# State-space stage of a hybrid decoder layer: groups pipelined four buffers deep, and its output stored with channels on rows

## The chip, the cores and the metric

The kernel runs on one core of one Trainium2 chip. The metric is the device time of one execution in microseconds (us). "TensorE" is the matrix engine (PE in the profile, PEld its weight loads), "VectorE" is DVE, "ScalarE" ACT, "GpSimd" POOL, and "SP" the queue that issues most transfers.

## What is computed

One step of a decoder layer: attention, an S5 state-space group and memory attention, each gated, then one output projection and a final norm. The change concerns the state-space part and the stage that reads its output:

```
for each of 24 groups g (16 channels, 64 complex states), 4096 positions l:
    h[l] = lam_bar[g] * h[l-1] + b_bar[g] @ u[l, g]          # complex
    y[l, g] = real(c[g] @ h[l]) + d_skip[g] * u[l, g]
s = gelu(y)                                                  # 4096 x 384
s = s * sigmoid(s @ w_glu + b_glu) * silu(gate_s)
x = x + concat(a, s, m) @ w_out ;  y_prompt = rmsnorm(x)
```

Eight sample rows (one token each) go through the same steps beside the prompt.

## The kernel before, in words

The kernel is a row of blocks, each with one program per engine, ordered by semaphores; the next block begins when all engines have ended the last. Two blocks are touched: `ssm` (L1503 to L1739) and `mix_out` (L1937 to L2234). Between them lies `sample_attend` (attention of the sample rows).

**ssm.** Positions are cut into 512 chunks of 8 (`NCH`, `STEP`), so that a scan over chunks is one VectorE instruction. For a group, TensorE turns the input (L1701: four 128x128 transposes into a bank), makes the small matrices (L1705 to L1711: one transpose, eight products 16 columns wide, one transpose of the sample rows); below this is "turn". ScalarE copies both banks out (L1674 `ut`, L1676 `sm`). VectorE builds two matrices from `sm` (L1621 to L1623, "matrices"). TensorE drives the states (L1717, L1718: two products of 512 columns, "drive"). VectorE rotates (L1629, L1630, L1632), scans (L1634) and rotates back (L1638 `cg`, L1639 `sg`). TensorE reads out (L1724 to L1732: per 128 chunks three products, then small ones for the samples). ScalarE takes the bank through Gelu (L1680 to L1682). A float32 product of one operand pair is two TensorE instructions in the profile.

The loop runs over 12 pairs of groups with two buffers of everything. In a pair each engine does its work in the same order: both turns, both matrices, both drives, both scans, both read-outs; nothing of the next pair begins before. Gelu writes into one tile `ssm_y` with positions on partitions, and SP stores all of it at the end (L1585, 6 MB, 12 KB a run). SP, in order, loads inputs (L1567, L1568), tables (L1571) and matrices (L1574) of the next pair, each behind a wait for the buffer, and in the first eight pairs also the 16 page loads of one sample (L1452, L1453). GpSimd meanwhile works for eight samples through the cached keys (`past.work`, L1455 to L1500), independently of the groups; `sample_attend` needs its result.

**mix_out** works in 8 tiles of 512 positions, in this order on every engine:

```python
            ready(0, 0)
            with engine.Fori(0, NB // 2 - 1) as i:
                ready(2 * i + 1, 1)
                project(2 * i, 0)
                ready(2 * i + 2, 0)
                project(2 * i + 1, 1)
            ready(NB - 1, 1)
```

`ready` prepares the operand of a tile: SP loads five rows of attention and memory output, the gate and y (L2019 to L2022; one buffer of each, so it waits for the previous tile's last VectorE split, L2079). TensorE turns y from positions on 64 rows to channels on 128 (L2192: 48 instructions), ScalarE copies it out into `st` (L2141, 3 times), TensorE multiplies by `w_glu` (L2200, 18 instructions), ScalarE applies the sigmoid (L2145), VectorE multiplies twice (L2073, L2075) and both split the operand into a high and a low half (L2150, L2079). `project` is 192 TensorE instructions (L2211) on a tile prepared one step earlier, and VectorE, ScalarE, GpSimd add, norm and store. In SP's order the loads of tile n+1 come behind the four x loads of tile n-1 (L2027), of which the last waits until two of that projection's four quarters are added (L2095).

Of the kernel before, what the change touches and what calls it, by code (L numbers as in the profile page):

```python
# [32 lines left out]
ACT = mybir.ActivationFunctionType  # L33
# [1469 lines left out]
def ssm(nc, c, a, ssm_prompt, ssm_sample, past):  # L1503
# [3 lines left out]

    NB = 4
    with ExitStack() as s:
# [6 lines left out]
        y = sb("ssm_y", [P, NB, STEP, WS])  # L1521
        turns = sb("ssm_turns", [P, 2, O_R])
        gp = sb("ssm_gp", [P, 2, GPW - O_R])
        u = sb("ssm_u", [P, 2, NB, SC])
        us = sb("ssm_us", [8, 2, SC])
        ut = sb("ssm_ut", [P, 2, NCH])
        sm = sb("ssm_sm", [P, 2, 2 * SC + 8])
        toep = sb("ssm_toep", [P, 2, SC])
        wj = sb("ssm_wj", [P, 2, SC])
# [15 lines left out]
        g_in = [sem("ssm_in0"), sem("ssm_in1")]  # L1545
        u_in = [sem("ssm_u_in0"), sem("ssm_u_in1")]
        turns_in = [sem("ssm_turns_in0"), sem("ssm_turns_in1")]
# [3 lines left out]
        y_done, y_out = sem("ssm_y_d"), sem("ssm_y_out")  # L1551
        tail, tail_pe, ends, stored = sem("ssm_tail"), sem("ssm_tail_pe"), sem("ssm_ends"), sem("ssm_stored")
        block = s.enter_context(nc.Block())
        u_v = c.u_chunks.rearrange("b p (g w) -> g p b w", g=G)
        z_u = c.zs[:, CU:CU + WS].rearrange("b (g c) -> g b c", c=GC)

        @block.sync
        def _(sp):
            sp.dma_start(h0in, a["state_ssm"].rearrange("o b g p r -> (o b g) (p r)").rearrange("(t q) w -> q t w", q=96)
                         .rearrange("q t (p r) -> q t p r", r=2)).then_inc(h_in, 16)  # L1560
            with nc.allow_non_contiguous_dma(reason="two columns of each group"):
                sp.dma_start(ab[:], c.ssm_gp[:, :, O_A1:O_A1 + 2].rearrange("g p w -> p g w")).then_inc(h_in, 16)
            sp.wait_ge(zeroed, 1)
            def groups(i, with_past):
                for j in range(2):
                    sp.wait_ge(sm_tr, at(2, i, j - 1))
                    sp.dma_start(u[:, j], u_v[2 * i + j]).then_inc(u_in[j], 16)  # L1567
                    sp.dma_start(us[:, j, SC - GC:SC], z_u[2 * i + j]).then_inc(u_in[j], 16)  # L1568
                for j in range(2):
                    sp.wait_ge(cg_done, at(4, i, 2 * j - 2))  # L1570
                    sp.dma_start(turns[:, j], c.ssm_gp[2 * i + j, :, 0:O_R]).then_inc(turns_in[j], 16)  # L1571
                for j in range(2):
                    sp.wait_ge(y_done, at(2, i, j - 1))
                    sp.dma_start(gp[:, j], c.ssm_gp[2 * i + j, :, O_R:GPW]).then_inc(g_in[j], 16)  # L1574
                if with_past:
                    past.load_sample(nc, sp, a, i)


            sp.wait_ge(past.p_in, 16)
            with sp.Fori(0, past.nbs) as i:  # L1580
                groups(i, True)
            with sp.Fori(past.nbs, G // 2) as i:
                groups(i, False)
            sp.wait_ge(y_out, at(2, G // 2, 0))
            sp.dma_start(c.y_chunks.rearrange("b p t f -> p b (t f)"), y[:].rearrange("p b t f -> p b (t f)")).then_inc(stored, 16)  # L1585
# [5 lines left out]
            sp.wait_ge(stored, 64)  # L1591
# [7 lines left out]
        def _(dve):  # L1599
            dve.sem_inc(cg_done, 4)  # L1600
            dve.sem_inc(small, 2)
            dve.sem_inc(turned, 4)
            dve.sem_inc(toep_done, 2)
# [12 lines left out]
            with dve.Fori(0, G // 2) as i:  # L1616
                for j in range(2):
                    g = 2 * i + j
                    dve.wait_ge(sm_done, at(2, i, j + 1))
                    dve.wait_ge(y_done, at(2, i, j - 1))  # L1620
# [40 lines left out]

        @block.scalar
        def _(act):
            act.sem_inc(sm_done, 2)
            act.sem_inc(ut_done, 2)
            act.sem_inc(y_out, 2)
            with act.Fori(0, G // 2) as i:
# [641 lines left out]
```

## Time and profile before

| | us |
|---|---|
| median of 3 runs | 4104.67 (4100.36 to 4107.49) |
| span of the profiled execution | 4106.5 |
| TensorE busy in it | 3573.2 (87%) |
| VectorE, ScalarE, GpSimd busy | 1689.6, 1011.2, 651.6 |

The page gives no time of the profiled execution beside its span; the span lies 1.8 us above the median and inside the range of the runs. Times in the rows are us from the span's start. A timeline row is: start, length, engine, line, operation, out<-in, count, and in brackets the idle time before and what ended it. PEclk is the granted share of TensorE's full clock.

### The profile page before, as it was taken

The page shows a single profiled execution, that of the slowest core. Times are in us where ns is not written, and L with a number is a line of the kernel's source. Part 1 is how long each engine was busy: PE and PEld are TensorE (multiplying, and loading weights), DVE is VectorE, ACT ScalarE, POOL GpSimd, SP SyncE. Part 2 cuts the span into 40 slices and gives each one's busy share as a digit, 9 for nine tenths or more (in the row PEclk, how much of TensorE's full clock was granted, in tenths as well). Part 3 has the DMA queues.
Part 4 walks back from the last instruction along what each step waited for, and adds up shares of the span by engine and source line. Part 5 has one row for each costly group of instructions (what it writes and reads, how often), then busy time and mean ns, then how long its engine had stood idle before and what let it go on. Part 6 is the DMA issues. An engine that isn't in the chain of part 4 may idle for free. (4 is left out here: it accounts for less than half of the span.)

```text
span 4106.5 us, 45401 instructions
## 1 busy us (share of the span) xinstructions
PE 3573.2 (87%) x14504; PEld 2549.9 (62%) x14504; DVE 1689.6 (41%) x2594; ACT 1011.2 (25%) x1823; POOL 651.6 (16%) x1265
## 2 busy tenths in 40 slices
PE   5999999999968989989999999967777775498999
PEld 4987988979844555555555555534335652376766
DVE  4122122131117657465573746527625442323232
ACT  1102111121112443434334343423201110112120
POOL 0000000000027777700000000000036630000000
PEclk9998999989977999999999999988777676698989
DMA  3232232132231121210101001032245532332422
GB/s 103 93 118 82 78 134 81 55 132 91 74 71 47 67 68 48 79 40 16 38 20 34 21 19 27 8 120 54 49 143 175 170 97 92 119 115 92 122 85 72
DMA packets 234113, 323.61 MB, mean 79 GB/s; under 512 B 100548, under 2 KB 168812, under 8 KB 232372
## 3 DMA queue, kind: packets, MB, share of 16 engines
q1 hardware_dynamic: 184436, 203.79, 17.6%
q10 hardware_dynamic: 37584, 68.48, 4.5%
q0 software_dynamic: 11904, 48.87, 3.4%
q8 instruction: 112, 1.84, 0.2%
q14 instruction: 77, 0.63, 0.0%
HBM read 221.37 MB, written 99.61 MB: 78 GB/s over the span
## 5 line engine op out<-in xcount | busy, mean ns | idle before, releaser
L1011 PE MATMUL bank<-p,vone 128*128 128x512 f32 (+1 forms) x1728 | 861.9, 581 | 10.5 <-ACT p L958 9.9
L958 ACT ACTIVATE p<-bank,ncol 128x512 f32<-128x512 f32 (+1 forms) x864 | 562.1, 651 | 815.4 <-PE bank L1028 645.7
L1027 PE MATMUL bank<-qhi,kst 128*128 128x512 f32 (+1 forms) x864 | 644.2, 746 | 14.0 <-issue 12.6
L879 DVE TENSOR_REDUCE pm<-bank 128x1 f32<-128x512 f32 (+2 forms) x864 | 516.8, 640 | 261.0 <-PE bank L998 193.0
L1011 PEld LDWEIGHTS bank<-p,vone 128*128 128x128 f32 x1728 | 320.9, 198 | 73.6 <-issue 13.1
L478 DVE CAST whi<-wraw 128x3072 fp32r<-128x3072 f32 (+2 forms) x32 | 52.1, 1629 | 755.9 <-PE bank L539 755.9
L998 PE MATMUL bank<-kone,qone 66*128 66x512 f32 (+2 forms) x864 | 293.6, 412 | 59.8 <-DVE qlo L865 33.9
L539 PE MATMUL bank<-xhi,whi 128*128 128x512 f32 x832 | 332.0, 399 | 6.9 <-DVE xlo L504 6.9
L1028 PE MATMUL bank<-qlo,kone 66*128 66x512 f32 (+1 forms) x864 | 335.9, 389 | 0.0
L539 PE MATMUL bank<-xhi,wlo 128*128 128x512 f32 x832 | 331.3, 398 | 0.0
L539 PE MATMUL bank<-xlo,whi 128*128 128x512 f32 x832 | 330.9, 398 | 0.0
L1027 PEld LDWEIGHTS bank<-qhi,kst 128*128 128x128 f32 x864 | 169.3, 196 | 194.3 <-issue 163.3
L1028 PEld LDWEIGHTS bank<-qlo,kone 66*128 66x128 f32 x864 | 168.9, 196 | 177.7 <-issue 170.9
L539 PE MATMUL bank<-whi,xlo 128*128 128x384 f32 (+1 forms) x768 | 278.5, 363 | 0.0
L539 PE MATMUL bank<-whi,xhi 128*128 128x384 f32 (+1 forms) x768 | 277.5, 361 | 0.0
L539 PE MATMUL bank<-wlo,xhi 128*128 128x384 f32 (+1 forms) x768 | 277.5, 361 | 0.0
L892 DVE RECIPROCAL rec<-bank 64x512 f32<-64x512 f32 x48 | 161.2, 3359 | 230.1 <-PE bank L1011 229.0
L998 PEld LDWEIGHTS bank<-kone,qone 66*128 66x128 f32 x864 | 165.6, 199 | 110.1 <-issue 49.1
L2211 PE MATMUL bank<-wo_hi,mx_hi 128*128 128x512 f32 x512 | 205.1, 401 | 0.8 <-DVE wo_raw L2117 0.8
L2211 PE MATMUL bank<-wo_lo,mx_hi 128*128 128x512 f32 x512 | 202.5, 396 | 0.0
L2211 PE MATMUL bank<-wo_hi,mx_lo 128*128 128x512 f32 x512 | 202.5, 396 | 0.0
L570 ACT ACTIVATE fstage<-bank 128x512 f32<-128x512 f32 x104 | 62.2, 598 | 508.4 <-PE bank L539 508.3
(390 smaller groups left out, 4970.7 us busy)
## 6 DMA issues: line engine op xcount, KB each, us to landing
wraw<-in_w_in SPq DMA_DIRECT2D x20, 1536.0 KB, 6.8
ssm_consts<-gp POOLq DMA_DIRECT2D x6, 3080.0 KB, 10.0
x_tok<-in_x_prompt SPq DMA_DIRECT2D x8, 2048.0 KB, 12.6
gate_t<-fstage ACTq DMA_DIRECT2D x32, 512.0 KB, 2.6
mx_x<-in_x_prompt SPq DMA_DIRECT2D x32, 512.0 KB, 3.5
out_y_prompt<-mx_xo ACTq DMA_DIRECT2D x32, 512.0 KB, 2.9
q<-q_t SPq DMA_DIRECT2D x96, 128.0 KB, 3.1
past_k<-in_cache_k POOLq DMA_DIRECT2D x64, 192.0 KB, 3.3
```

Source lines behind the costliest of these rows:

```text
L478: dve.tensor_copy(whi[:, si % 2, :, 0:w], wraw[:, :, 0:w]).then_inc(whi_done, 1)
L539: last = pe.matmul(dst, lhsT, rhs, start=(k == 0 and ws is whi and xs is xhi), stop=(k == KD - 1 and ws is wlo))
L570: act.activation(fstage[:, slot, 512 * h:512 * (h + 1)], bank[:], func, scale=1.0 if scale is None else scale).then_inc(evac_done, 1)
L879: dve.tensor_reduce(pm[:, r, ch:ch + 1], c.bank[XB + n % NPRE][:, 0:w], AX.X, ALU.max).then_inc(pre_max, 1)
L892: dve.reciprocal(rec[:], ob[HD:P, :]).then_inc(o_rec, 1)
L958: act.activation(p[:, n % 3, q0:512], c.bank[n % SB][:, q0:512], ACT.Exp, bias=ncol[:, j:j + 1]).then_inc(ex, 1)
L998: mm = pe.matmul(bank[:, 0:w], qone[:, b % QS, q], kone[:, 512 * ch:512 * ch + w], start=True, stop=True)
L1011: pe.matmul(c.bank[OB + b % 2][:, q0:512], vone[:, j, :], p[:, n % 3, q0:512], start=(j == 0), stop=(j == 4 * b + 3), skip_group_check=Tru ...
L1027: pe.matmul(bank[:, q0:512], kst[:, j * P:(j + 1) * P], qhi[:, b % QS, q0:512], start=True, stop=False)
L1028: mm = pe.matmul(bank[:, q0:512], kone[:, j * P:(j + 1) * P], qlo[:, b % QS, q0:512], start=False, stop=True)
L2211: mm = pe.matmul(c.bank[4 + 2 * (t % 2) + h][:], ms_[:, j, k, t * P:(t + 1) * P], ws_[:, k, 512 * h:512 * (h + 1)], start=(k == 0 and ws_ ...
```

## The change

In `ssm` every tile that SP fills, and those that `turn` and `matrices` make, get four buffers instead of two. The loop runs over quads, one group a step, and the engines' work of different groups is interleaved: TensorE in step g does drive(g+1), turn(g+2), read-out(g). Matrices(g+2) stand in VectorE's program between the first rotation of g and its scan. The two one-column copies (L1641, L1642) move to ScalarE. The read-out has the weights stationary, three products of 512 columns with channels on the output's rows; its Gelu goes to `yb` (two buffers), and SP stores each group (2 KB runs) into a new tensor `y_t` of shape (384, 4096). Two samples' page loads stand in each of the first four quads, one behind each odd group. `mix_out` loads `st` from `y_t` directly, in three transfers with runs of 64 values, positions inside a tile in the order (t, c) instead of (c, t); the second multiplication (L2075) restores the order, into a new tile `sn`. The transposes, the copies and the tile `mx_y` go. Core of the diff; in `ssm`, SP:

```diff
+            def quad(i, more, with_past):
+                for j in range(BUF):
+                    g = BUF * i + j
+                    sp.wait_ge(y_done, g + 1 + Y0)
+                    if more:
+                        load(g + BUF, j)
+                    sp.wait_ge(y_out, g + 1 + O0)
+                    sp.dma_start(y_v[g], yb[:, j % 2]).then_inc(y_st[j % 2], 16)
+                    if with_past and j % 2:
+                        past.load_sample(nc, sp, a, 2 * i + j // 2)
...
-            sp.dma_start(c.y_chunks.rearrange("b p t f -> p b (t f)"), y[:].rearrange("p b t f -> p b (t f)")).then_inc(stored, 16)
```

VectorE (`matrices` waits for `sm_done` of the group it is called with, by ScalarE's `take`):

```diff
+            def step(i, j, more):
+                g, q = BUF * i + j, j % 2
+                dve.wait_ge(turns_in[j], 16 * (i + 1))
+                dve.wait_ge(v_done, g + 1)
+                dve.tensor_tensor(vc[:, q], c.bank[4][:], cosT, M).then_inc(turned, 1)
+                dve.tensor_tensor(vs[:, q], c.bank[5][:], sinT, M).then_inc(turned, 1)
+                dve.wait_ge(turned, 2 * g + 2)
+                dve.tensor_tensor(vr[:, q], vc[:, q], vs[:, q], A_).then_inc(scanned, 1)
+                dve.wait_ge(y_done, g - 1 + Y0)
+                if more:
+                    matrices(g + 2, (j + 2) % BUF)
+                dve.wait_ge(scanned, 2 * g + 1)
+                dve.tensor_tensor_scan(gs[:, q], gp[:, j, O_R8 - O_R:O_R8 - O_R + 1].to_broadcast([P, NCH]), vr[:, q], 0.0, M, A_
+                                       ).then_inc(scanned, 1)
+                dve.wait_ge(small, g + 1)
+                dve.tensor_tensor(cg[:, q, 1:NCH + 1], cosT, gs[:, q], M).then_inc(cg_done, 1)
+                dve.tensor_tensor(sg[:, q, 1:NCH + 1], sinT, gs[:, q], M).then_inc(cg_done, 1)
```

ScalarE (`take` copies `ut` and `sm` out of their banks):

```diff
+            def step(i, j, more):
+                g, q = BUF * i + j, j % 2
+                if more:
+                    act.wait_ge(y_done, g - 1 + Y0)
+                    take(g + 2, (j + 2) % BUF)
+                act.wait_ge(cg_done, 2 * g + 2)
+                act.activation(hl[:, 0, bass.ds(g, 1)], cg[:, q, NCH:NCH + 1], ACT.Copy)
+                act.activation(hl[:, 1, bass.ds(g, 1)], sg[:, q, NCH:NCH + 1], ACT.Copy).then_inc(small, 1)
+                act.wait_ge(y_done, g + 1 + Y0)
+                act.wait_ge(y_st[q], 16 * (BUF // 2 * i + j // 2 + 1))
+                act.activation(vsm[:, :, bass.ds(g, 1)], c.bank[7][:, 0:8].unsqueeze(2), ACT.Copy)
+                act.activation(yst[:, bass.ds(g, 1), :], c.bank[7][0:GC, 16:24].unsqueeze(1), ACT.Gelu)
+                act.activation(yb[:, q], c.bank[6][:], ACT.Gelu).then_inc(y_out, 1)
```

TensorE:

```diff
+            def read_out(g, b):
...
+                pe.matmul(c.bank[6][:], toep[:, b], ut[:, b], start=True, stop=False)
+                pe.wait_ge(cg_done, 2 * g + 2)
+                pe.matmul(c.bank[6][:], w1, cg[:, b % 2, 0:NCH], start=False, stop=False)
+                pe.matmul(c.bank[6][:], w2, sg[:, b % 2, 0:NCH], start=False, stop=True).then_inc(y_done, 1)
+            def step(i, j, more, next_):
+                if next_:
+                    pe.wait_ge(turned, 2 * g + 2)
+                    drive(g + 1, (j + 1) % BUF)
+                if more:
+                    pe.wait_ge(sm_done, g + 1)
+                    turn(i + (j + 2) // BUF, g + 2, (j + 2) % BUF)
+                read_out(g, j)
```

In `mix_out`, SP, VectorE and TensorE:

```diff
-                sp.dma_start(yc[:], y_v[n]).then_inc(in_, 16)
+                for k in range(NKS):
+                    sp.dma_start(st[:, k].rearrange("p (t c) -> p t c", t=STEP), y_v[n, k]).then_inc(in_, 16)
...
-                    dve.tensor_tensor(sig[:, k], sig[:, k], gate[:, k], M).then_inc(s_done, 1)
+                    dve.tensor_tensor(sn[:, k].rearrange("p (c t) -> p c t", t=STEP), sig[:, k].rearrange("p (t c) -> p c t", t=STEP),
+                                      gate[:, k].rearrange("p (c t) -> p c t", t=STEP), M).then_inc(s_done, 1)
...
-                    for t in range(STEP):
-                        tr = pe.matmul(c.bank[k % 2][:, t * HD:(t + 1) * HD], yc[:, t, k * P:(k + 1) * P], c.ident[0:HD, 0:HD],
-                                       start=True, stop=True)
-                    tr.then_inc(tr_done, 1)
-                pe.wait_ge(st_done, NKS * n + NKS)
+                pe.wait_ge(in_, LOADS * n + LOADS)
+                pe.wait_ge(lo_done, at(KD, n, 0))
```

## Rows read from the trace of the kernel before

**Rows 1.** Windows: us of PE, PEld, DVE, ACT, POOL; PEclk; DMA share; GB/s.
```profile
3053.00:3387.00 334.00, 254.16 (x1303) 196.26 (x1301) 163.94 (x267) 55.58 (x138) 194.69 (x275) 0.75 0.50 146
3208.00:3235.00 27.00, 22.41 (x99) 17.26 (x100) 11.15 (x21) 4.05 (x9) 18.07 (x28) 0.62 0.56 159
3610.00:3678.00 68.00, 63.96 (x263) 48.28 (x263) 20.52 (x32) 14.02 (x23) 2.25 (x4) 0.90 0.33 105
```
**Rows 2.** Waits, 3025 to 3390 us: the read-out's (total, times, longest).
```profile
PE bank L1724 <- DVE ssm_sg L1639: 49.4, 20, 4.5
```
**Rows 3.** Timeline of POOL, state-space stage: its last instruction.
```profile
3330.90 0.21 POOL L1486 TENSOR_TENSOR past_qk<-past_k 128x12 f32<-128x12 f32 x1 [0.18 <-POOL past_k L1486]
```
**Rows 4.** Timeline: a group's turn (first, last), then VectorE's matrices (first, last).
```profile
3107.59 0.63 PE L1701 MATMUL bank<-ident,ssm_u 128*128 128x128 f32 x4 [0.42 <-issue]
...
3109.95 0.22 PE L1711 MATMUL bank<-ident,ssm_us 8*128 8x8 f32 x1
...
3110.63 0.35 DVE L1621 SCALAR_TENSOR_TENSOR ssm_toep<-ident,ssm_gp,ssm_sm 128x128 f32<-128x128 f32 x1 [1.92 <-ACT ssm_sm L1676]
...
3111.00 0.19 DVE L1623 TENSOR_SCALAR ssm_wj<-ssm_sm 128x64 f32<-128x64 f32 x1
```
**Rows 5.** Timeline after POOL's end: VectorE's scan, and TensorE's read-out that waits.
```profile
3347.44 1.22 DVE L1634 TENSOR_TENSOR_SCAN ssm_vs<-ssm_gp,ssm_vc 128x512 f32<-128x512 f32 x1
...
3350.04 0.39 PE L1724 MATMUL bank<-ssm_sm 128*128 128x8 f32 x2 [1.24 <-DVE ssm_sg L1639]
```
**Rows 6.** Groups by line, 3025 to 3390 us: busy us, mean ns.
```profile
L1634 DVE TENSOR_TENSOR_SCAN ssm_vs<-ssm_gp,ssm_vc 128x512 f32<-128x512 f32 x24 | 34.1, 1420 | 0.8
L1638 DVE TENSOR_TENSOR ssm_cg<-ssm_turns,ssm_vs 128x512 f32<-128x512 f32 x24 | 28.2, 1176 | 0.8
L1639 DVE TENSOR_TENSOR ssm_sg<-ssm_turns,ssm_vs 128x512 f32<-128x512 f32 x24 | 22.8, 948 | 0.0
...
L1621 DVE SCALAR_TENSOR_TENSOR ssm_toep<-ident,ssm_gp,ssm_sm 128x128 f32<-128x128 f32 x24 | 14.3, 595 | 147.7 <-ACT ssm_sm L1676 147.7
```
**Rows 7.** The tile ssm_y: its first and last evacuation by ScalarE.
```profile
L1682 ACT ACTIVATE ssm_y<-bank x24: 597/597/597, 3066.3 to 3381.1; 128x512 f32 x24
```
**Rows 8.** SP: a sample's 16 page loads (first, last); landing of L1574.
```profile
3106.19 0.36 SPq L1452 DMA_DIRECT2D past_v<-in_cache_v  x1
...
3119.13 0.34 SPq L1453 DMA_DIRECT2D past_lf<-in_cache_logf  x1
...
DMA to landing us min/median/max: 2.6/3.6/9.2
```
**Rows 9.** Timeline of SP: end of the state-space stage, first load of the next.
```profile
3381.68 0.41 SPq L1585 DMA_DIRECT2D y_chunks<-ssm_y  x1
...
3385.68 1.19 SPq L1589 DMA_DIRECT2D out_ssm_sample<-ssm_u  x1
3399.42 0.30 SPq L1792 DMA_DIRECT2D at_z<-z_sample  x1
```
**Rows 10.** Timeline, output stage: transposes, then GLU, between two projections.
```profile
3632.31 3.78 PE L2192 MATMUL bank<-ident,mx_y 64*128 64x64 f32 x32
...
3643.81 10.93 PE L2200 MATMUL bank<-mx_st,w_glu 128*128 128x512 f32 x18 [1.17 <-ACT mx_st L2141]
...
3651.15 0.19 PEld L2200 LDWEIGHTS bank<-mx_st,w_glu 128*128 128x128 f32 x1 [0.24 <-issue]
...
3653.72 0.19 PEld L2200 LDWEIGHTS bank<-mx_st,w_glu 128*128 128x128 f32 x1 [0.24 <-issue]
...
3654.18 0.80 PE L2211 MATMUL bank<-wo_hi,mx_hi 128*128 128x512 f32 x1
```
**Rows 11.** SP's first load for the next tile; the y tile's issue-to-landing times.
```profile
3611.48 0.38 SPq L2019 DMA_DIRECT2D mx_am<-mix_t  x1
...
DMA to landing us min/median/max: 10.7/14.9/18.8
```
**Rows 12.** Windows as in 1: transfers in runs of 256 bytes and less.
```profile
1216.00:1220.00 4.00, 1.12 (x4) 0.72 (x4) 3.59 (x7) 0.00 (x0) 3.43 (x8) 0.50 1.42 163
```

More of the change, by code:

```diff
@@ L1579, in _, with load @@
[L1579 to L1585 removed]
+            def load(g, b):
+                sp.dma_start(u[:, b], u_v[g]).then_inc(u_in[b], 16)
+                sp.dma_start(us[:, b, SC - GC:SC], z_u[g]).then_inc(u_in[b], 16)
+                sp.dma_start(gp[:, b], c.ssm_gp[g, :, O_R:GPW]).then_inc(g_in[b], 16)
+                sp.dma_start(turns[:, b], c.ssm_gp[g, :, 0:O_R]).then_inc(turns_in[b], 16)
@@ L1586, in _ @@
+            for j in range(BUF):
+                load(j, j)
+            sp.wait_ge(past.p_in, 16)
+            with sp.Fori(0, past.nbs // 2) as i:
+                quad(i, True, True)
+            for i in range(past.nbs // 2, LASTQ + 1):
+                quad(i, i < LASTQ, False)
+            for j in range(2):
+                sp.wait_ge(y_st[j], 16 * (G // 2 + 1))
             sp.dma_start(c.ys_t.rearrange("(g c) b -> c g b", c=GC), yst[:]).then_inc(stored, 16)
@@ L1644, in _ @@
+            for j in range(2):
+                matrices(j, j)
+            with dve.Fori(0, LASTQ) as i:
+                for j in range(BUF):
+                    step(i, j, True)
+            for j in range(BUF):
+                step(LASTQ, j, j < 2)
             bc = [P, 8, G]
-            dve.wait_ge(y_out, at(2, G // 2, 0))
+            dve.wait_ge(y_out, G + O0)
             dve.tensor_tensor(hn[:], h0[:], ab[:, :, 0].unsqueeze(1).to_broadcast(bc), M).then_inc(tail, 1)
@@ L1685, in _ @@
+            for j in range(2):
+                take(j, j)
+            with act.Fori(0, LASTQ) as i:
+                act.activation(table[:], c.minus_half[:, 0:1], ACT.Gelu)
+                for j in range(BUF):
+                    step(i, j, True)
+            for j in range(BUF):
+                step(LASTQ, j, j < 2)
         @block.tensor
         def _(pe):
-            pe.sem_inc(y_done, 2)
-            pe.sem_inc(sm_tr, 2)
+            pe.sem_inc(y_done, Y0)
             pe.wait_ge(prep, 6)
@@ L1733, in _, with turn @@
-            pe.wait_ge(small, at(2, G // 2, 0))
+            def turn(i, g, b):
+                pe.wait_ge(u_in[b], 32 * (i + 1))
+                pe.wait_ge(g_in[b], 16 * (i + 1))
+                for n in range(NB):
+                    tr = pe.transpose(c.bank[b % 2][:, n * P:(n + 1) * P], u[:, b, n, :], c.ident[:])
+                tr.then_inc(ut_tr, 1)
+                small_b = c.bank[2 + b % 2]
+                pe.transpose(small_b[:, 0:SC], gp[:, b, 0:SC], c.ident[:])
+                for t in range(STEP):
+                    w0 = (STEP - 1 - t) * GC
+                    pe.matmul(small_b[:, SC + t * GC:SC + (t + 1) * GC], gp[:, b, w0:w0 + SC], gp[:, b, O_CC - O_R:O_CC - O_R + GC],
+                              start=True, stop=True)
+                pe.transpose(small_b[:, 2 * SC:2 * SC + 8], us[:, b, :], c.ident[0:8, 0:8]).then_inc(sm_tr, 1)
@@ new lines, in step @@
+            def step(i, j, more, next_):
+                g = BUF * i + j
+                if next_:
[5 more added lines that the diff above has]
+                read_out(g, j)
+            for j in range(2):
+                turn(0, j, j)
+            drive(0, 0)
+            with pe.Fori(0, LASTQ) as i:
+                for j in range(BUF):
+                    step(i, j, True, True)
@@ L1734, in _ @@
+            for j in range(BUF):
+                step(LASTQ, j, j < 2, j < BUF - 1)
+            pe.wait_ge(small, G + 2)
             pe.wait_ge(tail, 4)
```

184 lines of the change are left out of this document (54 added, 130 removed).

## The prediction, made before the changed kernel was run

> **What bounds the kernel now.** I read the page first: TensorE is busy 87% of the span, so it bounds most of it, and only stretches where it waits, or does work that can go, are worth a change. The windows by stage find them. In the state-space stage TensorE is busy for 254 of 334 us at a mean granted clock of 0.75 [rows 1]: it stops and, in its busy time, often runs at the lower of its two levels (1.2 of 2.4 GHz). VectorE is busy for 164, GpSimd for 195: no engine fills the stage, a chain does. The waits name it: the read-out stands 49.4 us behind VectorE's last rotation [rows 2], because a pair runs turn, matrices, drive, scan, read-out one after the other. From the first Gelu to the last are 314.8 us for 23 groups, 13.7 each [rows 7]. GpSimd's own work ends at 3331.1 [rows 3], 50 us before the groups do, so it is hidden now and is the next floor.
>
> The stage's end shows the second place. SP issues the 6 MB store of y when all is done, and the next block's first load comes 17.7 us later [rows 9].
>
> In the output stage TensorE is busy for 94% of a tile's time [rows 1]; there each instruction taken from it is time. Between two projections lie 21.9 us: 11.5 from the first transpose to the GLU products (work and waits for ScalarE's copies), then 10.4 of GLU, whose first products run at the low clock [rows 10].
>
> **The change, part by part. The groups' loop.** It removes the pair's barriers, but the new order is a ring, not a free pipeline. Matrices(g+2) stand ahead of scan(g) in VectorE's program and need turn(g+2), which TensorE makes only after drive(g+1). One step at full clock: drive, four passes at 0.43 (six passes lie between the two weight loads of [rows 10]), 1.72; turn 2.58 [rows 4]; ScalarE's copy with its hand-offs 0.46 and matrices 0.56 [rows 4]; scan, rotation back and TensorE's start 2.60 [rows 5]; the two last 512-column products of the read-out 1.72. Together 9.64, of which 6.02 is TensorE. The rest of VectorE's step (2.1 for the forward rotation) and the product with `toep` lie beside it.
>
> Two corrections. While GpSimd works, VectorE's operations on SBUF are longer: scan 1.42 for 1.22, the rotations back 1.18 and 0.95 for 0.69, the first matrix 0.60 for 0.35 [rows 4 to 6]: 1.20 on average over 24 groups, of which some 21 fell in GpSimd's time, so 1.4 in those. And TensorE still waits in each step, at full clock for 3.62 less the first product and small ones, so the clock will not stay up. Its bounds are 1.0 and the 0.62 of the worst stretch of this stage [rows 1]; I take 0.75, the stage's own, since the new step has the same kinds of work and again a wait. Then a step is 6.02 / 0.75 + 3.62 + 1.4 = 13.0. From the first Gelu, taken to stay where it is, 21 steps of 13.0 and two short ones (no turn; no drive) of about 5 are 283, against 314.8: **32 saved**, with ends of -4 (a step of 14.7, below) and some 49 (a step under 11; GpSimd then ends the stage, below).
>
> What is moved: the two one-column copies leave VectorE for ScalarE, which idles and runs them beside the read-out: nothing. SP gets a store a group: 24 issues of about 0.4 [rows 9], and in the first 16 groups two groups cost it 16 page loads, 13.3 us [rows 8], and ten further issues, some 6: 19 of 26 us, so SP has room. But it is in order: behind an odd group's page loads the next group's inputs go out some 3 us late, and land 3.6 later, at most 9.2 [rows 8]; they are wanted about a step and a drive, 15 us, after their buffer came free. Covered at 13.0; at a step under 11 SP is the cover that goes. Gelu waits for the store two groups back, 26 us earlier: covered by the same margin. The deeper buffers cost nothing in themselves.
>
> **The stage's end.** With y stored group by group, what is left is the chain to the last store: its issue ends 5.2 after the last Gelu [rows 9], landing 3.6 (median of a 258 KB load [rows 8]): 8.8 instead of 17.7, **9 saved**, between 3 (landing 9.2) and 10 (2.6).
>
> **The output stage.** At six boundaries (tiles 2 to 7) transposes and copies go, and GLU begins where the projection ended, on an engine that had no gap: 18 passes at 0.43 are 7.7, instead of 21.9. That is 14.2 each, **85**; if GLU ran at half the clock, 15.5, it would be 38. ScalarE stores the last quarter before its first sigmoid, some 5 us after the boundary, as the copies wait now; GLU's third product needs a sigmoid at that time, so no stall of size. Tile 1 has no projection ahead of it: 11.5 of transposes go, and SP's two additional issues come on top, about 1.1: **10**. Tile 0 lies beside the splitting of the output weights on VectorE: 0, up to 11. The second multiplication reads with a stride of 64 values; VectorE is idle for two thirds of the stage [rows 1], so even twice its time is hidden.
>
> The cover of all this is the loads of tile n+1. Their first issue comes 20.8 us before the projection's end [rows 10, 11]; y is the fourth, 1.7 later, and lands 14.9 after that in the median: 4.2 to spare. The three new loads move the same 768 KB in runs of 256 bytes. I bound them by nothing, and by the 163 GB/s that short runs got elsewhere [rows 12], 4.8 us if none of it overlapped. With 1.1 for the issues this is 1.1 to 5.9 later, so between 3.1 to spare and 1.7 late. I take no wait: present y rows go to 64 partitions only, the new ones to 128, so the upper end counts a transfer that replaces one as if it were added.
>
> The Trainium skill (DMA: Bandwidth & Descriptors, Specifications) speaks against this part: under 512 bytes a run misses line rate, since the engine reads, modifies and writes. An estimate by the page, taking that as double work on the 163, is 9.6 us for y, and the sum would lose 6.5 at each of seven tiles, some 46.
>
> **Sum.** 32 + 9 + 85 + 10 = 136. The profiled span, 4106.5, lies 1.8 above the median; taken from the median, 4104.7 - 136 = **3969**.
>
> **The rivals. GpSimd becomes the end.** If the clock rises with the denser work, a step is about 11 (9.64 + 1.4) and the groups end near 3310; the block then ends with GpSimd, at 3331, or some 10 later if VectorE's denser work slows it as it now slows VectorE. The next block begins near 3342 instead of 3399.4: 58 for 41, and **3952**. It decides at a step below about 12.5. For it: TensorE's share of a step rises. Against: the wait in each step, and SP.
>
> **The ring gives nothing.** The change would then not do what it says: groups overlap in the program, but each step is as long as half a pair. At clock 0.62 the step is 6.02 / 0.62 + 3.62 + 1.4 = 14.7, the loop loses 4, the end still gains 9: **4005**. For it: a stretch at 0.62 exists, and eight instructions of 16 columns stand in every turn. Against: the barriers between pairs are gone.
>
> **Late y loads.** They take the 5.9 of the bound on top of the slowest landing so far, 18.8 for 14.9 [rows 11]: 5.6 late at tiles 1 to 7, 39 lost, **4008**. For it: the short runs. Against: 4.2 to spare in the median, and rows on 128 partitions.
>
> **Slower than before: the same loads, far later.** One mechanism: the 3072 short runs a tile drain so slowly that TensorE waits at seven boundaries for more than it saves. It decides at 136 / 7 = 19.4 us a tile behind the slack of 3.1, which is 768 KB at some 35 GB/s on top of what moves now. At 25 us: 7 x 25 - 136 = 39 lost, **4144**. For it: no row of before shows these runs from this tensor. Against: short runs at 163 GB/s [rows 12].
>
> **How the numbers follow.** Forecast 0.50, with its own range of 3953 to 3985; GpSimd's end 0.20; the ring without gain 0.15; late loads 0.10; slower 0.03; parts that cancel to within 0.2% (8 us, about what a measurement of this kernel can tell from no change) 0.02. The range takes in the first four: from 3940, where GpSimd's end has a faster tile 0 beside it, to 4015. Faster: all but the last two, 0.95.
>
> **What would show it.** Right: a Gelu every 13 us, the first rotation back directly behind matrices of two groups on; GpSimd's end still before the groups'; the next block 9 after the last Gelu; GLU products directly behind the last projection product, 7.7 long, with no wait for a DMA. Wrong: steps of 14 and more, or below 12 with GpSimd last; a wait of TensorE for `mx_st` loads of several us at each tile; ScalarE or SP as what ends the read-out's wait.

## The result, and the profile after

The changed kernel takes 3958.24 us (median of 4 runs, 3954.73 to 3964.21) against 4106.08 for the kernel before: a ratio of 0.9628, 95% interval 0.9605 to 0.9652. The forecast was 3969, with a range of 3940 to 4015. The profiled execution has a span of 3953.1 us. One execution of the last kernel below (v2_ring_pages_first) took 6225.22 us, at a granted clock of 0.77 where the others had 0.92, and is left out of its median.

First the state-space stage. The source view of the Gelu line: 24 groups, shortest, median and longest duration in ns, then first and last start.

```profile
L1698 ACT ACTIVATE ssm_yb<-bank x24: 571/571/575, 3059.0 to 3341.5; 128x512 f32<-128x512 f32 x24
```

From first to last are 282.5 us, where [rows 7] had 314.8. The 21 full steps take 272.7, or 12.99 each; the two short ones take 5.2 and 4.6. The first Gelu is also 7.3 us earlier. The windows view from first to last Gelu, columns as in [rows 1]:

```profile
3059.00:3342.00 283.00, 216.84 (x826) 121.82 (x824) 139.13 (x198) 51.53 (x168) 189.17 (x270) 0.76 0.63 185
```

TensorE is granted 0.76 of its clock and idles for 66 us. The waits of the stage (3025 to 3375; total us, times, longest) name the reason:

```profile
DVE ssm_toep L1621 <- ACT ssm_sm L1683: 152.2, 24, 7.7
...
POOL past_k L1464 <- issue: 73.7, 64, 3.2
PE bank L1749 <- DVE ssm_sg L1644: 65.9, 23, 5.0
```

The wait for the rotation back is longer than in [rows 2], not shorter. One step in the timeline shows the ring:

```profile
3161.51 1.02 PE L1737 MATMUL bank<-ssm_ut,ssm_sm 128*128 128x512 f32 x2
...
3163.77 1.86 PE L1730 MATMUL bank<-ssm_gp 128*128 128x16 f32 x16
...
3165.82 0.39 ACT L1683 ACTIVATE ssm_sm<-bank 128x264 f32<-128x264 f32 x1 [1.36 <-PE bank L1732]
...
3166.24 0.35 DVE L1621 SCALAR_TENSOR_TENSOR ssm_toep<-ident,ssm_gp,ssm_sm 128x128 f32<-128x128 f32 x1 [6.17 <-ACT ssm_sm L1683]
...
3166.71 1.22 DVE L1639 TENSOR_TENSOR_SCAN ssm_vs<-ssm_gp,ssm_vc 128x512 f32<-128x512 f32 x1
...
3168.57 0.69 DVE L1644 TENSOR_TENSOR ssm_sg<-ssm_turns,ssm_vs 128x512 f32<-128x512 f32 x1
...
3169.31 2.07 PE L1749 MATMUL bank<-ssm_cg,ssm_gp 128*128 128x512 f32 x2 [1.96 <-DVE ssm_sg L1644]
...
3171.18 1.91 PE L1750 MATMUL bank<-ssm_sg,ssm_gp 128*128 128x512 f32 x2
3172.89 1.92 PE L1737 MATMUL bank<-ssm_ut,ssm_sm 128*128 128x512 f32 x2
```

Drive, turn, ScalarE's copy, VectorE's matrices, scan, rotation, the last two products, next drive: each waits for the one before. From drive to drive this step takes 11.4 us; the operations of VectorE shown are as short in it as without GpSimd's work (see e3_no_products), and the mean of 12.99 has longer ones. VectorE stood idle for 6.17 us with a scan ready to run, because the matrices of two groups on come first in its program. The end of the stage on GpSimd, and on SP the next block's first load (timelines; answers to [rows 3] and [rows 9]):

```profile
3336.87 1.07 POOL L1486 TENSOR_TENSOR past_qk<-past_k 128x12 f32<-128x12 f32 x1 [0.18 <-POOL past_k L1486]
```

```profile
3349.18 0.29 SPq L1830 DMA_DIRECT2D at_z<-z_sample  x1
```

GpSimd ends at 3337.9, 3.6 us before the last Gelu. The next block starts 7.7 us after that Gelu (18.4 before), so 50.2 us earlier in all. The profiles of the experiments tell who ends the stage: the next block's first load comes 7.7 to 7.8 us after the last Gelu where the groups end it (here and in e3, e4, e5, e9 and e10), and 6.5 us after GpSimd's last instruction where GpSimd does (e1, e2, v1 and v2).

Then the output stage. TensorE's timeline at a boundary of steady tiles, where [rows 10] had 21.9 us:

```profile
3560.16 0.40 PE L2238 MATMUL bank<-wo_lo,mx_hi 128*128 128x512 f32 x1
3560.39 5.31 PE L2227 MATMUL bank<-mx_st,w_glu 128*128 128x512 f32 x12
3566.75 2.84 PE L2227 MATMUL bank<-mx_st,w_glu 128*128 128x512 f32 x6 [1.04 <-ACT mx_sig L2181]
3569.03 0.79 PE L2238 MATMUL bank<-wo_hi,mx_hi 128*128 128x512 f32 x1
```

GLU starts directly behind the projection and takes 8.64 us. SP's loads for it, and TensorE's waits in the whole stage (answers to [rows 11]):

```profile
3539.66 0.38 SPq L2058 DMA_DIRECT2D mx_am<-mix_t  x1
...
3541.34 10.66 SPq L2062 DMA_DIRECT2D mx_st<-y_t  x3
```

```profile
PE bank L2227 <- DMA mx_st<-y_t: 45.3, 2, 22.7
PE bank L2227 <- ACT mx_sig L2181: 7.0, 6, 1.4
```

The loads of y cause two waits, at tiles 0 and 1, and none in the steady tiles. The stage, from its first load to the end of the span, is 102.4 us shorter.

### The profile page after: what moved, and what is told of

Its sections match the earlier page's. It is cut to its first block and busy times, and to the rows that moved or that the text cites. A ratio compares the mean times of both kernels' runs of the same rounds, so it can differ in the third digit from the quotient of the medians.

```text
span 3953.1 us, 43519 instructions
## 1 busy us (share of the span) xinstructions
PE 3467.9 (88%) x13688; PEld 2412.2 (61%) x13688; DVE 1684.8 (43%) x2546; ACT 984.9 (25%) x1833; POOL 657.1 (17%) x1265
## 5 line engine op out<-in xcount | busy, mean ns | idle before, releaser
L1011 PE MATMUL bank<-p,vone 128*128 128x512 f32 (+1 forms) x1728 | 863.6, 581 | 10.7 <-ACT p L958 10.1
L998 PE MATMUL bank<-kone,qone 66*128 66x512 f32 (+2 forms) x864 | 293.7, 412 | 59.6 <-DVE qlo L865 33.6
L998 PEld LDWEIGHTS bank<-kone,qone 66*128 66x128 f32 x864 | 166.2, 200 | 109.5 <-issue 50.2
```

The costliest lines, as they stand in the source:

```text
L998: mm = pe.matmul(bank[:, 0:w], qone[:, b % QS, q], kone[:, 512 * ch:512 * ch + w], start=True, stop=True)
L1011: pe.matmul(c.bank[OB + b % 2][:, q0:512], vone[:, j, :], p[:, n % 3, q0:512], start=(j == 0), stop=(j == 4 * b + 3), skip_group_check=Tru ...
```

## The experiments

My theory after the result: the new order of the groups, a ring of 13.0 us, carries the gain of the state-space stage, with GpSimd as the floor just below. Its rivals: the deeper buffers carry it; or the ring sets nothing. For the output stage: the loads are hidden in steady tiles, with 2 to 3 us to spare. All times of the stage in one table; "first to last" is the Gelu's first and last start, and the waits are counted between them. Three more profiles with the changed kernel's state-space stage (e5, e6 and e7 below) have 284.5, 285.1 and 282.0 us from first to last, so a difference of some 3 us in that column tells nothing. A time marked * is a single run.

| kernel | first to last, us | TensorE's waits for `ssm_gp` loads | time of the kernel, us |
|---|---|---|---|
| before | 314.8 | 4.1 | 4106.1 |
| changed | 282.5 | none of size | 3958.2 |
| pairs, four buffers (e1_pairs) | 266.9 | none of size | 3953.4 |
| pairs, four buffers, first products late (e10_toep_late) | 283.4 | none of size | 3963.8* |
| pairs, two buffers (e9_two_buffers) | 318.0 | 22.6 | 3989.3* |
| matrices last (e2_matrices_last) | 229.1 | 25.3 | 3956.4 |
| no GpSimd products (e3_no_products) | 260.5 | none of size | 3936.7* |
| both (e4_both) | 233.0 | 32.1 | 3904.3* |
| matrices last, early page numbers (v1_ring_pages) | 239.0 | 33.6 | 3913.0 |

**The order alone undone (e1_pairs).** On TensorE, and likewise on the other engines:

```diff
-                for j in range(BUF):
-                    step(i, j, True, True)
+                for j in range(0, BUF, 2):
+                    for x in range(2):
+                        turn(i, BUF * i + j + x, j + x)
+                    for x in range(2):
+                        drive(BUF * i + j + x, j + x)
+                    for x in range(2):
+                        read_out(BUF * i + j + x, j + x)
```

> Only the pipelining is undone: each engine again works through a pair of groups (transposes of both, drives of both, scans of both, read-outs of both); the four buffers, the earlier loads, the store per group and the new output stage stay. Theory (the order of the steps carries the gain of the stage): first Gelu at 3059 as in the changed kernel, then 315 us to the last as in the kernel before, so the last at 3374 and the next block 32 us later: 3958 + 32 = 3990 us, from 3985 to 3995. Rival (the deeper buffers and earlier loads carry half of it): 299 us from first to last Gelu, 3974 us.

It is not slower: 3953.41 us, ratio 0.9614 (0.9596 to 0.9633), where the theory had 3990. The interval overlaps that of the changed kernel; the difference shows in the stage. Its Gelu line, its window from first to last Gelu, and its waits in the same stretch:

```profile
L1696 ACT ACTIVATE ssm_yb<-bank x24: 571/571/572, 3059.2 to 3326.1; 128x512 f32<-128x512 f32 x24
```

```profile
3059.00:3327.00 268.00, 216.29 (x848) 123.69 (x848) 154.33 (x201) 52.80 (x172) 184.04 (x259) 0.82 0.64 195
```

```profile
DVE ssm_toep L1621 <- ACT ssm_sm L1681: 92.1, 22, 7.6
...
PE bank L1751 <- DVE ssm_sg L1642: 22.6, 15, 2.6
```

The changed kernel's wait for the rotation back, also from first to last Gelu:

```profile
PE bank L1749 <- DVE ssm_sg L1644: 64.7, 22, 5.0
```

TensorE is busy as long as in the changed kernel (216.3 for 216.8 us), but waits for the rotation back 22.6 us instead of 64.7. So the pipelined order costs 15.6 us of the stage against pairs; it does not gain. Both theory and rival fall: the old order with the rest of the change is faster than either had it. The last Gelu comes 15.4 us earlier than in the changed kernel, the next block's first load only 4.7 (3344.5), because GpSimd then ends the stage, at 3338.1.

**The ring broken (e2_matrices_last).**

```diff
-                dve.wait_ge(y_done, g - 1 + Y0)
-                if more:
-                    matrices(g + 2, (j + 2) % BUF)
                 dve.wait_ge(scanned, 2 * g + 1)
...
                 dve.wait_ge(small, g + 1)
+                dve.wait_ge(y_done, g - 1 + Y0)
                 dve.tensor_tensor(cg[:, q, 1:NCH + 1], cosT, gs[:, q], M).then_inc(cg_done, 1)
                 dve.tensor_tensor(sg[:, q, 1:NCH + 1], sinT, gs[:, q], M).then_inc(cg_done, 1)
+                if more:
+                    matrices(g + 2, (j + 2) % BUF)
```

> VectorE makes the matrices of group g+2 after the second product of group g instead of ahead of its scan, so that the scan no longer waits for ScalarE's copy of the small matrices. Theory (the ring over TensorE, ScalarE and VectorE sets 13.0 us a step, and GpSimd, done at 3336.9, is the floor just below it): a step falls to 8 to 11 us, the last Gelu comes by 3310 or sooner, the wait of the scan for ScalarE (152 us) goes, and the block then ends with GpSimd at 3337 to 3345, so the next block's first issue comes 0 to 9 us earlier: 3949 to 3958 us. Rival (the ring does not set the step; TensorE's clock, SP's queue or the DMA engines do): steps stay at 12.5 to 13 and the time at 3958.

Ratio 0.9620 (0.9607 to 0.9633), 3956.40 us: inside the theory's band, as are the step and the last Gelu. Its Gelu line, the waits from first to last Gelu, and GpSimd's last instruction:

```profile
L1698 ACT ACTIVATE ssm_yb<-bank x24: 571/571/575, 3063.1 to 3292.2; 128x512 f32<-128x512 f32 x24
```

```profile
DVE ssm_toep L1621 <- ACT ssm_sm L1683: 69.4, 19, 11.2
...
PE bank L1723 <- DMA ssm_gp<-ssm_consts: 25.3, 8, 7.1
...
PE bank L1749 <- DVE ssm_sg L1642: 1.7, 1, 1.7
```

```profile
3346.29 0.21 POOL L1486 TENSOR_TENSOR past_qk<-past_k 128x12 f32<-128x12 f32 x1 [0.18 <-POOL past_k L1486]
```

TensorE's wait for the rotation falls from 64.7 to 1.7 us, a step from 13.0 to 10.4 (21 steps in 218.1 us). VectorE's wait for the copy does not go, though the theory had it gone (69.4 us), but TensorE no longer waits behind it. The last Gelu comes 49 us earlier, and the kernel gains nothing that can be told, because GpSimd now ends the stage, at 3346.5. Most of its later end is a later start: its first transfer of the stage is issued at 3032.1 in this profile and at 3025.7 in the changed kernel's. From there to its end it takes 314.4 us, for 312.3 there and 309.0 to 311.2 in e5, e6 and e7. The next block's first load comes 3.8 us later than in the changed kernel's profile (3353.0), not earlier. The next wait is the one for `ssm_gp` loads, 8 times: SP issues them behind 16 page loads.

**GpSimd's products and sums left out, alone and with the ring broken (e3_no_products, e4_both).**

```diff
-                pool.tensor_tensor(k, k, self.q[:].unsqueeze(1).to_broadcast([P, CP, WF]), ALU.mult).then_inc(self.summed, 1)
+                pool.sem_inc(self.summed, 1)
+                pool.wait_ge(pace, 3 * b + ch * 3 // NCK + 1)
...
-                    pool.tensor_tensor(out, kv[:, :, :, 0:w], kv[:, :, :, w:2 * w], ALU.add).then_inc(self.summed, 1)
+                    pool.sem_inc(self.summed, 1)
```

> Left out: GpSimd's products and sums over the cached keys (the scores are set to zero); its page loads stay, paced by the groups. Theory (contention with GpSimd's tensor operations costs VectorE's part of the ring 1.4 us a step): a step takes 11.6 us, the last Gelu is at 3059 + 21 x 11.6 + 10 = 3313, the scan takes 0.95 us again instead of 1.2, and the time is 28 us less, 3930. Rival (no contention on the path): steps stay at 13, 3958 us.

> Both edits together: matrices after the second product, and GpSimd's products and sums left out. Theory: with neither the ring nor GpSimd, a step is TensorE's own 6.02 / 0.75 = 8.0 us or the DMA engines' time for a group's loads (busy 0.73 of 13 us, so some 9.5), hence 8 to 10 us a step, the last Gelu at 3240 to 3280 and the time at 3860 to 3900. Rival (something else holds the step, as SP's queue): steps of 11 us or more, over 3915.

Without GpSimd's products and sums a step takes 11.93 us (21 steps in 250.5; 11.6 expected) and the one run 3936.74 us (3930 expected), so contention costs 1.06 a step where the prediction had 1.4. VectorE's groups of the changed kernel from first to last Gelu (count, busy us, mean ns, idle before), and those of e3_no_products:

```profile
L1639 DVE TENSOR_TENSOR_SCAN ssm_vs<-ssm_gp,ssm_vc 128x512 f32<-128x512 f32 x23 | 28.0, 1215 | 0.2
L1643 DVE TENSOR_TENSOR ssm_cg<-ssm_turns,ssm_vs 128x512 f32<-128x512 f32 x23 | 25.6, 1113 | 0.8
L1644 DVE TENSOR_TENSOR ssm_sg<-ssm_turns,ssm_vs 128x512 f32<-128x512 f32 x23 | 25.5, 1108 | 0.0
```

```profile
L1641 DVE TENSOR_TENSOR_SCAN ssm_vs<-ssm_gp,ssm_vc 128x512 f32<-128x512 f32 x23 | 28.1, 1220 | 0.2
L1645 DVE TENSOR_TENSOR ssm_cg<-ssm_turns,ssm_vs 128x512 f32<-128x512 f32 x23 | 15.9, 693 | 0.8
L1646 DVE TENSOR_TENSOR ssm_sg<-ssm_turns,ssm_vs 128x512 f32<-128x512 f32 x23 | 15.8, 686 | 0.0
```

In the ring it is the two rotations back that GpSimd lengthens (1113 for 693, 1108 for 686 ns); the scan does not change, though the expectation said it would. The Trainium skill (SBUF — State Buffer, SBUF: two separate sides) has the two engines take turns at a shared port pair that one of them holds for a whole instruction. The trace agrees for the rotations back, which read two tiles of SBUF; the forward products, which read a bank, take 680 and 677 ns beside GpSimd's work and 684 and 682 without. Which operation is lengthened goes with the order of the work, though: with the ring broken the scan is slower beside GpSimd too (e2_matrices_last, then e4_both):

```profile
L1636 DVE TENSOR_TENSOR_SCAN ssm_vs<-ssm_gp,ssm_vc 128x512 f32<-128x512 f32 x22 | 33.3, 1514 | 0.8
```

```profile
L1638 DVE TENSOR_TENSOR_SCAN ssm_vs<-ssm_gp,ssm_vc 128x512 f32<-128x512 f32 x22 | 26.9, 1224 | 0.7
```

With both edits a step is 10.7 us and the last Gelu starts at 3290.7, where the theory had 8 to 10 and 3240 to 3280; it was too low, and the rival's 11 or more is not reached either. The groups are no faster than with the ring broken alone (233.0 us for 229.1 in all), so GpSimd does not set that pace; but its floor is gone, and the kernel drops to 3904.3, just above the band expected. What is left of the step there shows in the waits: 32.1 us for `ssm_gp` loads.

**The buffers undone, and the earlier loads with them (e9_two_buffers).** e1_pairs with `BUF = 2`, each load behind the event that it had before (inputs after the turn, tables after the rotation, matrices after the read-out), and ahead of ScalarE's copies and VectorE's matrices the waits for an earlier read-out that two buffers need.

> The pairs of e1_pairs with two buffers of every tile again, and the loads where the kernel before has them (inputs behind the turn, tables behind the rotation back, matrices behind the read-out). Read-out, output and stores stay new. Theory after e1_pairs (the read-out's new form carries the gain of the stage: behind VectorE's last rotation stand two products of 512 columns instead of twelve of 128 columns and the small ones): the buffers are worth little, first to last Gelu 267 to 275 us as in e1_pairs (266.9). Rival (the deeper buffers and earlier loads carry it): 300 to 315 us, as in the kernel before.

The rival is the nearer one: 318.0 us, 3 above its band, and 3 above the kernel before, which has the old read-out. With two buffers, then, the rest of the new stage gains nothing. Its Gelu line, its window, its wait, and TensorE and SP around the end of one pair:

```profile
L1709 ACT ACTIVATE ssm_yb<-bank x24: 570/570/571, 3056.4 to 3374.4; 128x512 f32<-128x512 f32 x24
```

```profile
3056.00:3375.00 319.00, 253.66 (x849) 153.01 (x848) 146.30 (x201) 63.07 (x184) 188.96 (x274) 0.72 0.57 168
```

```profile
PE bank L1737 <- DMA ssm_gp<-ssm_consts: 22.6, 12, 2.7
```

```profile
3205.98 0.33 SPq L1587 DMA_DIRECT2D ssm_gp<-ssm_consts  x1
...
3206.30 1.02 PE L1765 MATMUL bank<-ssm_sg,ssm_gp 128*128 128x512 f32 x2
...
3209.99 1.09 PE L1737 MATMUL bank<-ident,ssm_u 128*128 128x128 f32 x4 [2.67 <-DMA ssm_gp<-ssm_consts]
...
3211.08 3.44 PE L1744 MATMUL bank<-ssm_gp 128*128 128x16 f32 x16
```

The next pair's matrices are asked for when the first read-out of a pair is done, and the second, now short, no longer covers their way. TensorE waits up to 2.7 us in each pair, and the granted clock is 0.72 where e1_pairs has 0.82: the same 848 instructions keep it busy for 253.7 us instead of 216.3. So of the 51.1 us between the two kernels 37.4 are TensorE's own work at a lower clock, the rest idle time. The slower work is what stands right behind the wait: from 3209.9 to 3223.2, both turns and the first drive, the granted clock is 0.50 to 0.52, the lower level, and the turn's 16 small instructions take 3.44 us, for 1.86 in the changed kernel's step above. From first to last Gelu these small instructions take 21.2 us more than in e1_pairs, the drives 13.7.

**The read-out's first products late again (e10_toep_late).** e1_pairs, with the wait for the rotated states ahead of the whole read-out:

```diff
                 pe.wait_ge(y_out, g + O0)
+                pe.wait_ge(cg_done, 2 * g + 2)
                 pe.matmul(c.bank[7][:, 0:8], sm[:, b, 0:SC], sm[:, b, 2 * SC:], start=True, stop=True)
...
-                pe.wait_ge(cg_done, 2 * g + 2)
```

> The pairs of e1_pairs, four buffers, but TensorE waits for the rotated states ahead of all products of the read-out, as the kernel before does, so that the product with toep and the small ones fall behind VectorE's last rotation again. Theory (what stands behind the rotation counts): two passes of 0.43 us at full clock or 0.86 at half, and some 0.5 for the small products, are added for each of 24 groups, 1.4 to 2.2 us each: first to last Gelu 267 + 33 to 53 = 300 to 320 us. Rival (buffers): 267 to 272 us.

Its Gelu line, TensorE's wait from first to last Gelu, and the window:

```profile
L1696 ACT ACTIVATE ssm_yb<-bank x24: 570/570/571, 3066.3 to 3349.7; 128x512 f32<-128x512 f32 x24
```

```profile
PE bank L1746 <- DVE ssm_sg L1642: 41.4, 15, 4.8
```

```profile
3066.00:3350.00 284.00, 215.28 (x848) 118.75 (x848) 161.24 (x199) 51.09 (x172) 191.81 (x273) 0.83 0.62 184
```

283.4 us lies below the theory's band and above the rival's. Having the product with `toep` and the small ones ahead of the wait is worth 16.5 us, 0.7 a group. Only 15 of the groups wait for the rotation, here as in e1_pairs, which fits that a part of it was covered in a pair anyway. TensorE's own work takes 215.3 us, as in e1_pairs (216.3): these waits are longer than those of e9_two_buffers and came with no lower clock (0.83, for 0.82 in e1_pairs).

**GpSimd's page numbers read early, ring broken (v1_ring_pages).** The edit of e2_matrices_last, and in GpSimd's program:

```diff
+                if ch + 2 < NCK or not last:
+                    pages = numbers(b + (ch + 2) // NCK, (ch + 2) % NCK)
                 w = HD
...
-                    load(b + (ch + 2) // NCK, (ch + 2) % NCK)
+                    load(ch, pages)
```

`numbers` holds the two reads of a page number into a register that stood ahead of the two transfers.

> The broken ring of e2_matrices_last, and GpSimd reads the page numbers of its next two loads while its products run instead of behind its sums. Theory (with the ring broken GpSimd alone ends the stage, and of its 300 us some 70 are waits ahead of its page loads, mostly for the page number): 40 to 60 us of these go, GpSimd ends at 3285 to 3310 instead of 3346, the groups at 3292 stay the end, and the time is 3905 to 3925 us. Rival (the wait is the issue itself or the page load): GpSimd ends where it did, 3956 us.

3912.96 us, ratio 0.9523 (0.9498 to 0.9548). GpSimd's waits in the stage now, and its last instruction:

```profile
POOL past_k L1467 <- POOL past_qk L1491: 22.2, 30, 0.8
...
POOL past_k L1467 <- issue: 4.9, 2, 3.8
```

```profile
3300.15 0.21 POOL L1491 TENSOR_TENSOR past_qk<-past_k 128x12 f32<-128x12 f32 x1 [0.18 <-POOL past_k L1491]
```

The 73.7 us ahead of the page loads (72.9 in e2_matrices_last) fall to 27.1. GpSimd takes 274.2 us from its first transfer, for 314.4 in e2_matrices_last, and ends 46 us earlier; the groups' earlier end, hidden until now, reaches the time. The last Gelu starts at 3296.1, so groups and GpSimd end within some 4 us of each other again, GpSimd last.

**Long runs (e6_long_runs), y loaded twice (e7_y_twice), y loaded first (e5_y_first).**

```diff
-        y_v = c.y_t.rearrange("(k p) (t n c) -> n k p t c", p=P, t=STEP, c=NCT)
+        y_v = c.y_t.rearrange("(k p) (n t) -> n k p t", p=P, t=TB)
```

> The output stage loads each tile of y in runs of 2 KB instead of 256 bytes; the order of the positions inside a tile, which the short runs restore, is left out. Theory (in the steady tiles the loads are hidden, and SP's 10 us for the three issues too; only tile 0 and tile 1, which start with no projection ahead of them, wait for them): the steady tiles keep their period of 54 us within 0.5, the two waits of TensorE for the y loads (45 us) fall by 6 to 12 us together, 3946 to 3952 us. Rival (the short runs delay steady tiles too): the period falls by over 1 us, 3940 us or less.

Steady tiles keep their period: SP's first loads of tiles 2 to 7 lie 53.8 to 54.1 us apart in both kernels. The second half of the theory fails: TensorE's two waits are 43.6 us for 45.3, and the one run took 3963.56 us, outside both bands. Its span is 8.9 us longer than the changed kernel's, and 6.6 of that lie ahead of the output stage, where nothing was changed. The output stage itself, from its first load to the end of the span, takes 501.5 us; in the eight profiles that have the changed kernel's output stage it takes 499.2 to 500.2. Long runs gave nothing. SP's issues are far shorter, and the same bytes land no sooner to speak of (10.0 us in the median after the issue, for 10.8). SP's timeline for one steady tile, to be set beside the 10.66 us above:

```profile
3546.93 2.36 SPq L2062 DMA_DIRECT2D mx_st<-y_t  x3
```

> Each tile's y is loaded twice, with the same short runs, the first time into a tile that nobody reads. Theory (in steady tiles the last y load lands 2 to 3 us ahead of the projection's end): the second set lands 9 to 12 us later, and TensorE waits 6 to 10 us for it at each of tiles 2 to 7 and about 10 more at tiles 0 and 1: 4010 to 4040 us. Rival (the loads are hidden with 10 us and more to spare): waits at tiles 0 and 1 alone, up to 3980 us.

The rival is right, at 3967.96 us: TensorE's waits in the stage stay at two, now 51.9 us.

```profile
PE bank L2230 <- DMA mx_st<-y_t: 51.9, 2, 28.8
```

Even 768 KB more in short runs for each tile fit ahead of the projection's end. The slack of 2 to 3 us that I had read off the DMA engines' busy time was too small.

e5_y_first issues the three loads of y ahead of the other three, with a semaphore of their own:

```diff
-                pe.wait_ge(in_, LOADS * n + LOADS)
+                pe.wait_ge(y_in, YLOADS * n + YLOADS)
```

> The three loads of y go out first of a tile's loads and count on a semaphore of their own, so that the products of the gate (GLU) wait for y alone; the rest is the changed kernel. Theory (only tiles 0 and 1 wait, behind loads that GLU does not read): GLU of these two starts 3 to 5 us earlier each, steady tiles stay at 54 us, the time falls by 4 to 9 us, 3949 to 3954. Rival (SP's 10 us for the three issues then delays the other loads, which the splitting needs at once): no gain, or 2 to 5 us a tile lost.

3952.46 us, ratio 0.9611 (0.9590 to 0.9631): inside the band, but the interval overlaps that of the changed kernel. The stage shows it: 492.5 us, for 499.2 to 500.2, and the two waits fall from 45.3 to 39.5 us. SP's timeline for one steady tile:

```profile
3548.44 3.45 SPq L2059 DMA_DIRECT2D mx_st<-y_t  x3
```

The same three loads in the same short runs now hold SP for 3.1 to 3.6 us in the steady tiles, for 8.9 to 10.7 in the changed kernel, and land 6.3 us after their issue in the median, for 10.8. So most of the issue time, and 4.5 us of the landing, came from standing behind the tile's other loads.

**All together (v2_ring_pages_first).**

> All three edits that may help: matrices after the second product, GpSimd's page numbers read beside its products, y loaded first. Theory: the 3913 us of v1_ring_pages less what y first gives, 3904 to 3910. Rival: 3913 us, the loads of y do not matter.

3904.38 us (median of five), ratio 0.9504 (0.9485 to 0.9523), 54 us below the changed kernel and inside the theory's band. Most of it is v1_ring_pages; the interval does not tell y's part from nothing, but the output stage takes 492.4 us here too, with 40.4 us in its two waits.

## Why the prediction was right, and where it was not

The number held, and the sum in its main terms: from span to span the loop gave 32.3 us (32 forecast), the stage's end 10.6 (9), the output stage 102.4 (95) and the earlier first Gelu 7.3 (nothing), 152.6 of the 153.4 between the two spans, where 136 were forecast. The reason given for one of its parts did not hold.

- **Groups' loop.** 13.0 a step and 283 us were forecast, 12.99 and 282.5 measured, at a granted clock of 0.76 (0.75 taken). The ring is real: broken in e2_matrices_last, a step takes 10.4. The contention term was 1.06, not 1.4, and the other terms 0.3 larger; that the two cancel is luck. Of the 1.06 the two rotations back are 0.84, and the scan, priced at 0.20, is nothing. That first rotation back follows matrices of two groups on is what the timeline shows.
- **What the loop's gain came from.** The step that failed is "It removes the pair's barriers, but the new order is a ring" as the origin of the 32 us, with "The deeper buffers cost nothing in themselves" as all that was said of the buffers. With the pairs kept, the rest of the change gives 266.9 us, 15.6 fewer than the pipelined order. Four buffers with their earlier loads give 51.1 (e9_two_buffers to e1_pairs); with four buffers the early products (`toep` and the small ones) are worth 16.5; with two, the new read-out and the stores by group together are worth nothing (318.0 for 314.8). I priced one new order against one old one and never the old order with the new buffers.
- **The ring gives nothing.** This rival's words, "each step is as long as half a pair", are nearer to the mechanism than its price: half a pair with the same buffers is 11.8 us (11 pairs in 259.0), a ring step 13.0.
- **GpSimd becomes the end.** It did not in the changed kernel (3337.9 against a last Gelu at 3341.5), by 3.6 us. It did in e1_pairs (half a pair 11.8) and e2_matrices_last (a step of 10.4), as "decides at a step below about 12.5" has it. That a denser VectorE slows it by some 10 us is not shown: from its first transfer GpSimd takes 305.0 us before, 309.0 to 312.3 in four profiles with the ring and 314.4 in e2_matrices_last, but its tensor operations take only some 3 us more there (170.6 for 167.5 before), the rest is in the waits ahead of its page loads. SP as "the cover that goes" at a step under 11 shows in the 25.3 us of waits for `ssm_gp`.
- **First Gelu "taken to stay where it is".** It came 7.3 us earlier (6.9 when counted from GpSimd's first transfer, and 7.1 to 7.2 so in e5, e6 and e7): the first group's matrices are now SP's third load of the loop, and TensorE's first turn starts at 3032.4 instead of 3042.1.
- **Stage end.** 7.7 us from the last Gelu to the next block's load; 18.4 before. 10.6 saved, 9 forecast.
- **Output stage.** 102.4 saved, 95 forecast. A boundary is 8.64 us, not 7.7, since "no stall of size" is a stall for the sigmoid at each of six, 1.04 at the one shown and 7.0 in all: 13.2 saved each, 79, for 85. Tile 0, "0, up to 11", gave 8.3: from its first load to that of tile 1 are 40.5 us, 48.8 before. So its transposes were hardly hidden beside the splitting of the weights, though no run takes them out alone. Tile 1 gave 12.6, for 10.
- **Loads of y.** No wait in steady tiles, as taken. The issues, "about 1.1" more for two, took some 10 us for the three, since they stand behind the tile's other loads (3.1 to 3.6 ahead of them, e5_y_first). In the steady tiles it did not matter; at tiles 0 and 1 the order was worth some 7 us. The Trainium skill (DMA: Bandwidth & Descriptors, Specifications) puts line rate at 512 bytes a run and above; by the prediction's estimate from it 46 us were at stake. Here e6_long_runs with 2 KB runs kept the period of the steady tiles, so the rule took nothing from this kernel's time; that it lengthens the transfer itself is not excluded, since the median landing differs by 0.8 us.

## What to carry to other kernels

A change that alters the order of the work and the depth of its buffers is two changes: price each with the other held, because the depth may carry the gain and the new order may cost some of it back. Here only the old order could be tried at both depths: the new one has turn(g+2) ahead of read-out(g), which still reads the buffers of g, so it needs more than two. In a software pipeline, place work for a later group behind the chain of the present one in each engine's program; ahead of it, it can close a ring, as here. A stage that two engines end within a few us may gain nothing from speeding up one alone (e2_matrices_last), unless that frees the other too (e3_no_products, 21 us); look at what the other spends outside its arithmetic.

## What the hardware showed that I had not expected

- **Register loads on GpSimd.** Reading its page numbers ahead of 64 loads held GpSimd for 73.7 us of waits in the changed kernel; with the numbers read while a tensor operation runs, the waits ahead of the same loads were 27.1 (v1_ring_pages), of which 22.2 were for its own sums.
- **Issue time on SP.** Three transfers of 256 KB in 256-byte runs held SP's queue for 10.66 us behind three other loads, with 2 KB runs for 2.36 at the same place, and ahead of the other loads, still in short runs, for 3.45 (e5_y_first). With the same loads issued twice (e7_y_twice) the first three took 8.8 to 10.7 us in the steady tiles, the second three 3.2 to 4.6. So it is not a fixed price a run: what stands ahead in the queue counts for more here. What sets it in detail stays open.
- **The cost of a wait went with its place.** In e9_two_buffers waits of at most 2.7 us (22.6 in all) stand ahead of the turns; turns and first drive then ran at the lower clock, and TensorE's work took 37.4 us more. In e10_toep_late waits of up to 4.8 us (41.4 in all) stand ahead of the read-out, and its work took no longer than in e1_pairs. What else the difference rests on, no run shows.
